# Three edits at three places of an eight-layer transformer kernel: one reciprocal for four heads, the second mixer's decayed scores moved later, and four items between scores and weights in attention

## The chip, the cores and the metric

The kernel is one program on one core of a Trainium2 chip. The metric is the device time of the whole program in microseconds (us), the median over several executions. A core has TensorE (PE, matrix products), VectorE (DVE), ScalarE (ACT), GpSimd (POOL) and SyncE (SP, which here only starts DMAs). Each engine takes its own instructions strictly in order and waits at semaphores for the others.

## The reference

Two stacks run one after the other on 256 tokens of width 1024. The first stack has two layers with 256 context tokens beside the 256 tokens, the second has four layers with 16 meta tokens ahead of them (272 tokens). Everything is float32. The three pieces that matter here, cut to their core:

```python
# first stack, layer 0, differential attention: one square sum over 128 values for each of 4 heads
def diff_post(o, subln_g, lam_init):
    o = rms_norm(o, subln_g, SUBLN_EPS) * (1.0 - lam_init)      # y = x * rsqrt(mean(x^2) + eps) * g

# first stack layer 1 (8 heads x 2 query blocks, 512 keys) and FoX attention (16 heads)
def fox_attend(q, cq, qpos, k, v, ck, kpos):
    s = jnp.einsum('bqhd,bkhd->bhqk', q, k) 
    s = jnp.where(kpos[None, :] <= qpos[:, None], s + (cq[..., :, None] - ck[..., None, :]), -jnp.inf)
    p = jax.nn.softmax(s, axis=-1)
    return jnp.einsum('bhqk,bkhd->bqhd', p, v)

# second stack, layer 1 (GLA): scores with a decay per channel
def gla_chunk(state, inputs):
    b = jnp.cumsum(g, axis=1)
    decay = jnp.exp(jnp.where(causal, b[:, :, None] - b[:, None, :], -jnp.inf))
    A = jnp.einsum('bthd,bshd,btshd->bhts', q, k, decay)
    ...
```

The second stack's layers are FoX, GLA, GDN, FoX, each followed by a gated feed-forward layer.

## The kernel before

The program is a list of stages (classes with one method per engine). Most stages multiply activations by streamed weights: a ring of six 1 MB slots is filled by SP, ACT copies the upper half of each float32 weight (L2034, two halves of 1.0 us), DVE forms the lower half (L2042), and PE does three products for each block (L2069). SP starts a slot's next load when PE has finished with its last content. Between most stages there is a barrier: the next stage's instructions on an engine wait until all three engines are through.

**Head norm.** `HeadNorm` runs after the first layer's attention, on four heads of 128 partitions x 512 tokens. For each head ACT squares (L690), PE sums over the partitions with a 128x128 matrix of ones, so that every partition gets the same row (L708), ACT takes the root (L696), DVE takes the reciprocal of all 128x512 values (L720) and scales the head (L730). Beside it PE and ACT do four slots of the modulation product (`ModSlots`: L409, L418, L436; the DVE ends them with L453 and L459). Then `OutNorm` begins, with ACT's split of the activations (L2129) and of its first weights (L2034, which ACT does ahead of the barrier), and PE's first product (L2069).

**Attention.** `Attention` works through a list of items in steps. An item is a head and a block of queries; it has `maps` (one product q.k, or two for the differential heads). In step i the engines do, each in its own order:

- PE: scores of item i (L803), transposes of the weights of item i-2 (L812), output product of item i-3 (L822);
- DVE: mask and maximum of item i (L857, L860, L869, L877), then reciprocal of the sum and scaling of the weights of item i-1 (L890, L894);
- ACT: exponential of item i (L924), copy of the transposed weights of item i-2 (L934), copy of the output of item i-3 (L940).

PE's scores of item i wait for the exponential of item i-2, since their PSUM banks are shared. Where the next stage is known (`follow`), ACT and DVE also do its splits at fixed steps (L2410, L2405, L2414, and three `upper` of L2034 in steps N-7, N-4 and N-1). There are four such stages: the first layer's (mixed items, with one and two maps), the second layer's (16 equal items of 512 keys), and FoX twice. In the first FoX stage the 48 items repeat in threes (the text calls them M, A and B: 16, 144 and 272 keys, with one, two and three blocks of transposes); in the second one the 32 items alternate A, B.

**GLA.** `GlaProject` multiplies by 12 weight slots, with 28 results (`items` 0 to 27), and hangs other work between them: after result i come `beside_tensor`, `beside_scalar` and `beside_vector` with that i. Results 8 to 19 are the values V, in threes of 16, 128 and 128 tokens, three to a slot. The decayed scores have eight levels, l = -1 to 6. For each level from 0 on DVE forms differences (`diff`, L3087, L3089), ACT exponentials (`decay`, L3013), DVE multiplies q and k by them (`scaled`, L3098), PE multiplies (`pairs`, L2910, L2914, L2917), and DVE keeps what belongs to the level (`kept`, L3110, L3112). The table `SCORES` says after which result a level's `pairs` stands; `diff` and `decay` stand two results ahead of it, `scaled` one ahead, `kept` one behind. `SPLIT_SLOTS` is 3: after the last result of a slot come the splits of the slot three later.

Of the kernel before, what the change touches and what calls it, by code (L numbers as in the profile page):

```python
# [18 lines left out]
ALU = mybir.AluOpType  # L19
# [715 lines left out]

class Attention(Stage):
# [21 lines left out]
    def ahead_scalar(self, act, step):  # L758
# [4 lines left out]
        for k in range(KC):  # L763
            if step == self.done(k) + 5:
# [3 lines left out]
    def ahead_vector(self, dve, step):  # L768
# [4 lines left out]
        for k in range(KC):  # L773
            if step == self.done(k) + 4:
                dve.wait_ge(self.scalar_done, self.act.at("out", self.done(k)))
                self.follow.split_times(dve, k)
            if step == self.done(k) + 6:
                self.follow.split_lo(dve, k)
# [5 lines left out]
    def bank(self, i, m):  # L784
        return (i % 2) * 2 + m
# [4 lines left out]
    def tensor(self, pe):  # L790
        c, N = self.c, len(self.items)
        ident = c.s("ident")
        for step in range(N + 3):
# [12 lines left out]
            if 2 <= step < N + 2:  # L806
                i, it = step - 2, self.items[step - 2]
# [3 lines left out]
                for b, (lo, n) in enumerate(self.blocks(it)):  # L811
                    tr = pe.transpose(c.ps[0:n, 4 + i % 2, b * P:b * P + it["rows"]],  # L812
                                      self.p[0:it["rows"], 2 * (i % 2), lo:lo + n], ident[0:it["rows"], 0:it["rows"]])
                tr.then_inc(self.tensor_done, self.pe.mark("turned", i))
            if step >= 3:
                i, it = step - 3, self.items[step - 3]
# [14 lines left out]
    def vector(self, dve):  # L831
# [5 lines left out]
        for step in range(N + 1):  # L837
            if self.mods and step == self.steps + 2:
                self.mods.finish(dve, self.dve)
            if step < N:  # L840
                i, it = step, self.items[step]
                R, K = it["rows"], it["keys"]
                for m in range(len(it["maps"])):
                    col = self.cols[0:R, self.bank(i, m), :]
                    dve.wait_ge(self.tensor_done, self.pe.at("scores", i, m))
                    if i >= 2:

                        dve.wait_ge(self.scalar_done, self.act.at("exp", i - 2, m if m < len(self.items[i - 2]["maps"]) else 0))
                        dve.wait_ge(self.vector_done, self.dve.at("weights", i - 2))
# [28 lines left out]
            if step >= 1:  # L878
                i, it = step - 1, self.items[step - 1]
# [12 lines left out]
                p0 = self.p[0:R, 2 * (i % 2), 0:K]  # L892
                col = self.cols[0:R, self.bank(i, 0), :]
                ins = dve.tensor_scalar(p0, p0, col[:, 6:7], None, ALU.mult)  # L894
                if M == 2:
                    ins.then_inc(self.vector_done, self.dve.mark("p0", i))
                    p1 = self.p[0:R, 2 * (i % 2) + 1, 0:K]
# [7 lines left out]
        if self.follow:  # L905
            for step in range(N + 1, N + 6):
                self.ahead_vector(dve, step)

    def scalar(self, act):
        c, N = self.c, len(self.items)  # L910
        for step in range(N + 3):
            if step < N:
                i, it = step, self.items[step]
                R, K = it["rows"], it["keys"]
                for m in range(len(it["maps"])):
                    col = self.cols[0:R, self.bank(i, m), :]
                    act.wait_ge(self.vector_done, self.dve.at("neg", i, m))
                    if i >= 2:
                        act.wait_ge(self.tensor_done, self.pe.at("turned", i - 2))
# [4 lines left out]
                    act.activation(self.p[0:R, 2 * (i % 2) + m, 0:K], src, ACT.Exp, bias=col[:, 2:3],  # L924
# [3027 lines left out]
```

## Time and the profile before

| | us |
|---|---|
| median of 3 runs | 3140.18 (3138.24 to 3140.91) |
| the profiled execution | 3141.45 |
| its span in the profile | 3139.6 |
| PE busy | 2833.6 (90%) |
| DVE busy | 2133.0 (68%) |
| ACT busy | 1574.0 (50%) |
| head norm, from its first instruction to PE's first product of the next stage | 22.1 (332.5 to 354.6) |
| second layer's attention | 43.9 (911.9 to 955.8) |
| first FoX attention | 95.8 (1482.2 to 1578.0), PE busy 80.7, DVE 69.3 |
| GLA from result 8 to the state's products | 60.1 (1845.5 to 1905.6), PE busy 48.9 |
| second FoX attention | 75.4 (2840.2 to 2915.6), PE busy 59.3, DVE 53.4 |

The profiled execution took 1.85 us more than its span, which lies around the span, and 1.27 us more than the median. The last five rows are stretches of the span, in us from its start. PE's busy time counts overlapping products, so that 90% is not PE at its peak. The span's forty slices show PE at eight or nine tenths from the seventh slice on, with a few dips; the places of the change lie in slices 5, 12 and 13, 19 to 21, 24 and 25, and 37 and 38.

### The profile page before, as it was taken

How to read it: one execution, taken by the hardware profiler on the slowest of the kernel's cores; microseconds unless marked ns; L12 is line 12 of the kernel's file. 1: busy time of each engine (PE TensorE's matmuls, PEld its weight loads, DVE VectorE, ACT ScalarE, POOL GpSimd, SP SyncE). 2: the span in 40 equal slices, each digit the busy share in tenths (PEclk: the TensorE clock that was granted, in tenths of full speed). 3: DMA queues.
4: the chain of work that ended last, by engine and by line, in shares of the span. 5: the costliest groups of instructions: out<-in, count | busy, mean ns of one | idle time of the engine just before them, and what ended most of it. 6: DMA issues, size and time to landing. Idle time of an engine off the chain costs nothing.

```text
span 3139.6 us, 56486 instructions
## 1 busy us (share of the span) xinstructions
PE 2833.6 (90%) x21486; PEld 2547.6 (81%) x21486; DVE 2133.0 (68%) x3895; ACT 1574.0 (50%) x2757; POOL 94.4 (3%) x92
## 2 busy tenths in 40 slices
PE   6988779997797999789899988999988899998999
PEld 4855559996656999778799978998878799897898
DVE  2167649886475899676767775677746577786676
ACT  3255348775444888654643354434732343455532
POOL 0000001110000011000000000000000000000000
PEclk9999879998798999889999999999989999999999
DMA  8262229999272999933045532454420155441453
GB/s 269 87 201 81 81 100 360 355 353 332 68 228 73 337 355 356 313 95 121 1 135 174 174 95 91 165 174 151 131 81 1 46 169 174 148 130 46 135 187 108
DMA packets 420405, 524.51 MB, mean 167 GB/s; under 512 B 14160, under 2 KB 386912, under 8 KB 419952
## 3 DMA queue, kind: packets, MB, share of 16 engines
q1 hardware_dynamic: 408336, 499.72, 48.1%
q0 software_dynamic: 9216, 12.61, 1.2%
q10 hardware_dynamic: 2656, 9.49, 0.8%
q8 instruction: 132, 2.16, 0.3%
q14 instruction: 65, 0.53, 0.1%
HBM read 521.71 MB, written 21.02 MB: 173 GB/s over the span
## 4 chain that ended last, share of the span: by engine, by line
PE 76%; DVE 10%; ACT 5%; DMA 5%; issue 3%; ACTq 0%; PEldq 0%; SPq 0%; DVEq 0%; PEld 0%; POOLq 0%
PE ps L2069 19%; PE ps L2557 6%; PE ps L2558 6%; PE ps L2559 6%; PE ps L1716 3%; PE ps L1715 3%; PE ps L1714 3%; PE ps L2577 3%; PE ps L2579 3%; PE ps L2578 3%; DMA ring<-in_w_down 2%; PE ps L803 2%; PE ps L822 2%; PE ps L1750 2%; PE ps L1752 2%
## 5 line engine op out<-in xcount | busy, mean ns | idle before, releaser
L1884 DVE TENSOR_TENSOR W_lo<-ring,W_hi 128x1024 fp32r<-128x1024 f32 x384 | 452.5, 1220 | 61.2 <-ACT W_hi L1801 58.4
L2069 PE MATMUL ps<-H_part,W_hi 128*128 128x272 f32 (+2 forms) x1800 | 418.6, 307 | 31.3 <-DVE H_part L1973 12.7
L1801 ACT ACTIVATE W_hi<-ring 128x1024 fp32r<-128x1024 f32 x384 | 385.1, 1053 | 77.8 <-DMA ring<-in_w_up 35.2
L2606 ACT ACTIVATE W_hi<-ring 128x1024 fp32r<-128x1024 f32 x264 | 263.0, 1049 | 293.9 <-PE ps L2579 185.4
L2557 PE MATMUL ps<-room_part,W_hi 128*128 128x272 f32 (+1 forms) x1408 | 404.4, 287 | 5.0 <-DVE room_part L1973 5.0
L2558 PE MATMUL ps<-room_part,W_hi 128*128 128x272 f32 (+1 forms) x1408 | 403.6, 287 | 0.0
L2559 PE MATMUL ps<-room_part,W_lo 128*128 128x272 f32 (+1 forms) x1408 | 402.8, 286 | 0.0
L2069 PEld LDWEIGHTS ps<-H_part,W_hi 128*128 128x128 f32 x1800 | 303.2, 192 | 54.0 <-issue 35.7
L2646 DVE TENSOR_TENSOR W_lo<-ring,W_hi 128x1024 fp32r<-128x1024 f32 x264 | 313.9, 1218 | 10.6 <-ACT W_hi L2606 9.6
L2069 PE MATMUL ps<-H_part,W_lo 128*128 128x272 f32 (+2 forms) x1024 | 305.1, 298 | 0.0
L2042 DVE TENSOR_TENSOR W_lo<-ring,W_hi 128x1024 fp32r<-128x1024 f32 x186 | 219.4, 1220 | 117.3 <-ACT W_hi L2034 116.5
L1714 PE MATMUL ps<-W_hi,A_split_hi 128*128 128x256 f32 x1024 | 293.6, 287 | 2.3 <-DVE A_split_lo L1890 2.3
L1716 PE MATMUL ps<-W_hi,A_split_lo 128*128 128x256 f32 x1024 | 290.5, 284 | 0.0
L1715 PE MATMUL ps<-W_lo,A_split_hi 128*128 128x256 f32 x1024 | 289.9, 283 | 0.0
L2689 DVE TENSOR_TENSOR X<-X,ps 128x272 f32<-128x272 f32 (+1 forms) x352 | 141.0, 428 | 198.5 <-PE ps L2579 196.6
L2557 PEld LDWEIGHTS ps<-room_part,W_hi 128*128 128x128 f32 x1408 | 265.1, 188 | 7.8 <-issue 7.1
L2559 PEld LDWEIGHTS ps<-room_part,W_lo 128*128 128x128 f32 x1408 | 265.1, 188 | 0.0
L2558 PEld LDWEIGHTS ps<-room_part,W_hi 128*128 128x128 f32 x1408 | 265.0, 188 | 0.1
L2034 ACT ACTIVATE W_hi<-ring 128x1024 fp32r<-128x1024 f32 x186 | 185.6, 1049 | 150.5 <-PE ps L2069 121.3
L2577 PE MATMUL ps<-room_part,W_hi 128*128 128x272 f32 (+1 forms) x704 | 205.5, 292 | 21.2 <-DVE W_lo L2646 21.2
L2579 PE MATMUL ps<-room_part,W_lo 128*128 128x272 f32 (+1 forms) x704 | 205.2, 291 | 0.0
L2578 PE MATMUL ps<-room_part,W_hi 128*128 128x272 f32 (+1 forms) x704 | 204.8, 291 | 0.0
(492 smaller groups left out, 6292.4 us busy)
## 6 DMA issues: line engine op xcount, KB each, us to landing
ring<-in_w_down SPq DMA_DIRECT2D x108, 1024.0 KB, 5.0
ring<-in_w_gate_up SPq DMA_DIRECT2D x88, 1024.0 KB, 5.1
ring<-in_w_gate SPq DMA_DIRECT2D x64, 1024.0 KB, 9.8
ring<-in_w_up SPq DMA_DIRECT2D x64, 1024.0 KB, 9.5
ring<-in_w_mod SPq DMA_DIRECT2D x48, 1024.0 KB, 5.8
ring<-in_fox_w_in SPq DMA_DIRECT2D x32, 1024.0 KB, 5.8
ring<-in_gdn_w_in SPq DMA_DIRECT2D x16, 1024.0 KB, 5.7
ring<-in_gla_w_in SPq DMA_DIRECT2D x12, 1024.0 KB, 6.2
```

Source lines behind the costliest of these rows:

```text
L1714: pe.matmul(out, xh, wh[:, k, :], start=(k == 0), stop=False)
L1715: pe.matmul(out, xh, wl[:, k, :], start=False, stop=False)
L1716: mm = pe.matmul(out, xl, wh[:, k, :], start=False, stop=(k == KC - 1))
L1801: act.activation(self.parts(p)[0][:, W], c.ring[:, g % SLOTS, W], ACT.Copy).then_inc(c.hi_done, 1)
L1884: dve.tensor_tensor(lo, c.ring[:, (self.g0 + p) % SLOTS, W], hi.bitcast(F32), ALU.subtract)\
L2069: mm = pe.matmul(self.out(i), a, b, start=(k == 0 and n_part == 0), stop=(k == KC - 1 and n_part == 2))
L2557: pe.matmul(out, wh[:, k, M], hi, start=(k == 0), stop=False)
L2558: pe.matmul(out, wh[:, k, M], lo, start=False, stop=False)
L2559: mm = pe.matmul(out, wl[:, k, M], hi, start=False, stop=(k == KC - 1))
L2577: pe.matmul(out, wh[:, k, M], ah, start=(k == 0), stop=False)
L2579: mm = pe.matmul(out, wl[:, k, M], ah, start=False, stop=(k == 1))
L2646: dve.tensor_tensor(lo, c.ring[:, (self.g0 + p) % SLOTS, C], hi.bitcast(F32), ALU.subtract)\
```

## The change

It does three things.

1. `HeadRoots` takes the place of `HeadNorm` after the first layer's attention. PE sums the squares of the four heads in 32-partition groups with a column of ones, so that one 128x128 tile holds all 4 x 512 sums; one root and one reciprocal of that tile follow; PE spreads the rows again to 128 partitions, four products of 128 columns for each head; DVE scales with the spread values in PSUM.
2. `Attention` gets `depth` and `lag`. Where all items have one map, `depth` is 4 and `lag` is 1: four PSUM banks and four weight buffers, PE's scores of item i wait for the exponential of item i-4, and in step i DVE scales the weights of item i-2 (not i-1), PE transposes those of i-3 (not i-2) and multiplies those of i-4 (not i-3), and ACT copies i-3 and i-4. The splits for the next stage stand one step later, the three `upper` where they were. The first layer's attention has items with two maps and keeps 2 and 0.
3. `GlaProject.SCORES` puts most levels one or two results later, and `diff` and `decay` stand three results ahead of `pairs`, `scaled` two.

```diff
+class HeadRoots(Stage):
+    HEADS, SIDE = 4, 4
...
+    def tensor(self, pe):
+        c = self.c
+        self.mods.tensor(pe, 0, self.HEADS)
+        pe.wait_ge(self.vector_done, self.dve.at("column"))
+        for h in range(self.HEADS):
+            pe.wait_ge(self.scalar_done, self.act.at("square", h))
+            for q in range(self.SIDE):
+                mm = pe.matmul(c.ps[32 * q:32 * q + 32, 0, 0:P], self.column[:, 31 - h:63 - h], self.sq[:, h, q * P:(q + 1) * P],
+                               start=(h == 0), stop=(h == self.HEADS - 1))
+        mm.then_inc(self.tensor_done, self.pe.mark("sums"))
+        self.mods.tensor(pe, 1, self.HEADS)
+        pe.wait_ge(self.vector_done, self.dve.at("root"))
+        for h in range(self.HEADS):
+            for q in range(self.SIDE):
+                one = c.s("ident")[:, 32 * q + h:32 * q + h + 1].to_broadcast([P, P])
+                mm = pe.matmul(c.ps[:, h, q * P:(q + 1) * P], one, self.root, start=True, stop=True)
+            mm.then_inc(self.tensor_done, self.pe.mark("spread", h))
+        self.mods.tensor(pe, 2, self.HEADS)
+        self.mods.tensor(pe, 3, self.HEADS)
+
+    def scalar(self, act):
+        c = self.c
+        for h, x in enumerate(self.heads):
+            act.activation(self.sq[:, h, :], x, ACT.Square).then_inc(self.scalar_done, self.act.mark("square", h))
+        self.mods.scalar(act, 0, self.HEADS)
+        act.wait_ge(self.tensor_done, self.pe.at("sums"))
+        act.activation(self.root, c.ps[:, 0, 0:P], ACT.Sqrt, bias=self.eps, scale=1.0 / (P * self.after ** 2))\
+           .then_inc(self.scalar_done, self.act.mark("root"))
+        for s in range(1, self.HEADS):
+            self.mods.scalar(act, s, self.HEADS)
...
+        dve.reciprocal(self.root, self.root).then_inc(self.vector_done, self.dve.mark("root"))
+        for h, x in enumerate(self.heads):
+            dve.wait_ge(self.tensor_done, self.pe.at("spread", h))
+            dve.scalar_tensor_tensor(x, x, self.gain, c.ps[:, h, :], ALU.mult, ALU.mult)
+        self.mods.finish(dve, self.dve)
...
+        single_maps = all(len(it["maps"]) == 1 for it in items)
+        self.depth, self.lag = (4, 1) if single_maps else (2, 0)
...
     def bank(self, i, m):
-        return (i % 2) * 2 + m
+        return i % 4 if self.depth == 4 else (i % 2) * 2 + m
...
-                if i >= 2:
-                    for m in range(len(self.items[i - 2]["maps"])):
-                        pe.wait_ge(self.scalar_done, self.act.at("exp", i - 2, m))
+                if i >= self.depth:
+                    for m in range(len(self.items[i - self.depth]["maps"])):
+                        pe.wait_ge(self.scalar_done, self.act.at("exp", i - self.depth, m))
...
-    SCORES = {8: -1, 9: 0, 10: 1, 12: 2, 13: 3, 15: 4, 16: 5, 18: 6}
+    SCORES = {9: -1, 11: 0, 12: 1, 14: 2, 15: 3, 16: 4, 17: 5, 19: 6}
...
-        l = self.SCORES.get(i + 2)
+        l = self.SCORES.get(i + 3)
...
-        l = self.SCORES.get(i + 1)
+        l = self.SCORES.get(i + 2)
```

**ACT in the second FoX stage, before.** An exponential (L924), the copy of transposed weights (L934, 256 columns for an item A, 384 for B) and the copy of an output (L940) are a step.

```order
1480 L924 ACTIVATE H,room<-H,room 128x272
1481 L934 ACTIVATE room<-ps 128x384
1482 L940 ACTIVATE room<-ps 64x128
1483 L924 ACTIVATE H,room<-H,room 128x144
1484 L934 ACTIVATE room<-ps 128x256
1485 L940 ACTIVATE room<-ps 64x128
```

And with the change (L987 is the exponential, L998 and L1005 the copies):

```order
1475 L987 ACTIVATE H,room<-H,room 128x144
1476 L998 ACTIVATE room<-ps 128x384
1477 L1005 ACTIVATE room<-ps 64x128
1478 L987 ACTIVATE H,room<-H,room 128x272
1479 L998 ACTIVATE room<-ps 128x256
1480 L1005 ACTIVATE room<-ps 64x128
```

The kinds of instructions stand in the same order as before. What moved is the item behind the exponential: the one of 272 keys is now followed by the copy of an item A, and the one of 144 keys by that of an item B.

**DVE in GLA, before.** It begins with the two instructions that form b (L3075, L3079).

```order
1817 L3075 SCALAR_TENSOR_TENSOR room<-room 128x1088
1818 L3079 SCALAR_TENSOR_TENSOR room<-room 128x1088
1819 L3087 TENSOR_TENSOR room<-room 128x1088 x2
1820 L3098 TENSOR_TENSOR ACC<-room 128x544 x2
1821 L3098 TENSOR_TENSOR ACC<-room 128x272x2 x2
1822 L3110 COPY_PREDICATED room<-ACC,ps 128x256
1823 L3112 COPY_PREDICATED room<-ACC,ps 16x64
1824 L2042 TENSOR_TENSOR W_lo<-ring,W_hi 128x1024 x2
```

And with the change (L3154 `diff`, L3165 `scaled`, L3177 and L3179 `kept`, L2107 the lower half of a weight slot):

```order
1813 L3142 SCALAR_TENSOR_TENSOR room<-room 128x1088
1814 L3146 SCALAR_TENSOR_TENSOR room<-room 128x1088
1815 L3154 TENSOR_TENSOR room<-room 128x1088 x2
1816 L3165 TENSOR_TENSOR ACC<-room 128x544 x2
1817 L2107 TENSOR_TENSOR W_lo<-ring,W_hi 128x1024 x2
1818 L3165 TENSOR_TENSOR ACC<-room 128x272x2 x2
1819 L3177 COPY_PREDICATED room<-ACC,ps 128x256
1820 L3179 COPY_PREDICATED room<-ACC,ps 16x64
```

The differences of levels 0 and 1 and the products of level 0 stand as before, but the weight slot's lower half is now ahead of the products of level 1 and of `kept` of level -1.

**DVE in the head norm with the change** (L786 the reciprocal, L789 the scaling, L453 and L459 the modulation's end); before it were four pairs of L720 and L730, each of 128x512, between L443 and L453.

```order
434 L781 MEMSET ACC 128x63
435 L783 MEMSET ACC 128x1
436 L442 MEMSET ps 128x256 x3
437 L443 TENSOR_REDUCE room<-small 128x2
438 L786 RECIPROCAL ACC<-ACC 128x128
439 L789 SCALAR_TENSOR_TENSOR room<-room,small,ps 128x512 x4
440 L453 TENSOR_TENSOR MOD<-ps,small 128x8 x2
```

One reciprocal of a quarter of the size of one before stands ahead of four scalings, which now read PSUM.

## Rows read from the trace of the kernel before

**Rows 1.** Timeline of the head norm: start us, us, engine, line; idle before in brackets.

```profile
333.79 1.28 ACT L696 ACT_TABLE_LOAD   x1
...
335.81 3.35 DVE L720 RECIPROCAL ACC<-ACC 128x512 f32<-128x512 f32 x1 [2.25 <-ACT ACC L696]
...
339.20 0.75 DVE L730 SCALAR_TENSOR_TENSOR room<-room,small,ACC 128x512 f32<-128x512 f32 x1
...
345.23 2.00 ACT L2034 ACTIVATE W_hi<-ring 128x1024 fp32r<-128x1024 f32 x2 [0.17 <-issue]
...
352.54 4.27 ACT L2129 ACTIVATE H_part<-room 128x512 fp32r<-128x512 f32 x8 [5.31 <-DVEq L3850]
...
354.63 0.77 PE L2069 MATMUL ps<-H_part,W_hi 128*128 128x512 f32 x1 [8.92 <-DVE room_part L2134]
```

**Rows 2.** The reciprocals of line L1085: ns min/median/max, forms.

```profile
L1085 DVE RECIPROCAL stat<-stat x4: 553/753/953, 415.0 to 1343.4; 128x128 f32<-128x128 f32 x2, 128x64 f32<-128x64 f32 x2
```

**Rows 3.** Timeline of PE in the second layer's attention.

```profile
923.45 1.02 PE L803 MATMUL ps<-room 128*128 128x512 f32 x2
...
924.75 1.05 PE L822 MATMUL ps<-room 128*128 128x128 f32 x8
...
925.64 1.02 PE L803 MATMUL ps<-room 128*128 128x512 f32 x2
```

**Rows 4.** Timeline of the second FoX attention, one loop.

```profile
2867.98 0.36 ACT L934 ACTIVATE room<-ps 128x256 f32<-128x256 f32 x1
...
2868.98 0.37 DVE L857 TENSOR_SCALAR H<-ps,room 128x144 f32<-128x144 f32 x1 [0.98 <-PE ps L803]
...
2870.29 0.52 ACT L924 ACTIVATE H<-H,room 128x272 f32<-128x272 f32 x1 [1.49 <-DVE room L877]
...
2870.81 0.47 ACT L934 ACTIVATE room<-ps 128x384 f32<-128x384 f32 x1
...
2871.34 0.94 PE L822 MATMUL ps<-room 128*128 128x128 f32 x6 [0.18 <-ACT room L934]
...
2872.11 0.62 PE L803 MATMUL ps<-ACC,room 128*128 128x272 f32 x2
...
2873.23 0.37 DVE L857 TENSOR_SCALAR H<-ps,room 128x144 f32<-128x144 f32 x1 [0.84 <-PE ps L803]
```

**Rows 5.** Timeline of the first FoX attention.

```profile
1504.40 0.23 DVE L857 TENSOR_SCALAR H<-ps,room 128x16 f32<-128x16 f32 x1
...
1508.66 0.41 PE L803 MATMUL ps<-ACC,room 128*128 128x144 f32 x2
...
1508.86 0.36 DVE L894 TENSOR_SCALAR H<-H,room 128x272 f32<-128x272 f32 x1
...
1509.36 0.23 DVE L857 TENSOR_SCALAR H<-ps,room 128x16 f32<-128x16 f32 x1
...
1510.48 0.23 DVE L894 TENSOR_SCALAR H<-H,room 128x16 f32<-128x16 f32 x1
```

**Rows 6.** Waits of PE over the span: us in total, times, longest.

```profile
PE ps L803 <- ACT H L924: 5.4, 2, 3.2
```

**Rows 7.** Timeline of GLA after result 8.

```profile
1852.19 2.49 DVE L3087 TENSOR_TENSOR room<-room 128x1088 f32<-128x1088 f32 x2
...
1856.25 1.08 PE L2910 MATMUL ps<-ACC 128*32 128x32 f32 x64 [6.73 <-DVE ACC L3098]
...
1863.01 0.41 PE L2069 MATMUL ps<-W_hi,H_part 128*16 128x256 f32 x2
...
1863.74 2.36 DVE L2042 TENSOR_TENSOR W_lo<-ring,W_hi 128x1024 fp32r<-128x1024 f32 x2 [5.56 <-ACT W_hi L2034]
...
1865.83 0.40 PE L2069 MATMUL ps<-W_hi,H_part 128*128 128x256 f32 x2
```

**Rows 8.** Waits of PE in GLA, 1845 to 1910.

```profile
PE ps L2910 <- DVE ACC L3098: 9.4, 3, 6.7
```

**Rows 9.** GLA by stretch: length, busy PE, PEld, DVE, ACT, POOL, granted clock, DMA.

```profile
1857.00:1861.00 4.00, 4.00 (x50) 3.96 (x41) 1.18 (x4) 0.00 (x0) 0.00 (x0) 0.50 0.02 4
```

More of the change, by code:

```diff
@@ L763, in ahead_scalar @@
         for k in range(KC):
-            if step == self.done(k) + 5:
+            if step == self.done(k) + 5 + self.lag:
                 act.wait_ge(self.scalar_done, self.act.at("out", self.done(k)))
@@ L773, in ahead_vector @@
         for k in range(KC):
-            if step == self.done(k) + 4:
+            if step == self.done(k) + 4 + self.lag:
                 dve.wait_ge(self.scalar_done, self.act.at("out", self.done(k)))
                 self.follow.split_times(dve, k)
-            if step == self.done(k) + 6:
+            if step == self.done(k) + 6 + self.lag:
                 self.follow.split_lo(dve, k)
@@ L805, in tensor @@
                     mm.then_inc(self.tensor_done, self.pe.mark("scores", i, m))
-            if 2 <= step < N + 2:
-                i, it = step - 2, self.items[step - 2]
+            i = step - 2 - self.lag
+            if 0 <= i < N:
+                it = self.items[i]
                 pe.wait_ge(self.vector_done, self.dve.at("weights", i))
@@ L812, in tensor @@
                     tr = pe.transpose(c.ps[0:n, 4 + i % 2, b * P:b * P + it["rows"]],
-                                      self.p[0:it["rows"], 2 * (i % 2), lo:lo + n], ident[0:it["rows"], 0:it["rows"]])
+                                      self.p[0:it["rows"], self.bank(i, 0), lo:lo + n], ident[0:it["rows"], 0:it["rows"]])
                 tr.then_inc(self.tensor_done, self.pe.mark("turned", i))
-            if step >= 3:
-                i, it = step - 3, self.items[step - 3]
+            i = step - 3 - self.lag
+            if i >= 0:
+                it = self.items[i]
                 pe.wait_ge(self.scalar_done, self.act.at("turned", i))
@@ L836, in vector @@
             self.mods.begin(dve)
-        for step in range(N + 1):
+        for step in range(N + 1 + self.lag):
             if self.mods and step == self.steps + 2:
@@ L877, in vector @@
                         dve.tensor_scalar(col[:, 2:3], col[:, 0:1], -scale, None, ALU.mult).then_inc(self.vector_done, self.dve.mark("neg", i, m))
-            if step >= 1:
-                i, it = step - 1, self.items[step - 1]
+            i = step - 1 - self.lag
+            if 0 <= i < N:
+                it = self.items[i]
                 R, K, M = it["rows"], it["keys"], len(it["maps"])
@@ L905, in vector @@
         if self.follow:
-            for step in range(N + 1, N + 6):
+            for step in range(N + 1 + self.lag, N + 6 + self.lag):
                 self.ahead_vector(dve, step)
@@ L910, in scalar @@
         c, N = self.c, len(self.items)
-        for step in range(N + 3):
+        for step in range(N + 3 + self.lag):
             if step < N:
@@ L927, in scalar @@
                 self.mods.scalar(act, step - 1, self.steps)
-            if 2 <= step < N + 2:
-                i, it = step - 2, self.items[step - 2]
+            i = step - 2 - self.lag
+            if 0 <= i < N:
+                it = self.items[i]
                 act.wait_ge(self.tensor_done, self.pe.at("turned", i))
@@ L935, in scalar @@
                    .then_inc(self.scalar_done, self.act.mark("turned", i))
-            if step >= 3:
-                i, it = step - 3, self.items[step - 3]
+            i = step - 3 - self.lag
+            if i >= 0:
+                it = self.items[i]
                 act.wait_ge(self.tensor_done, self.pe.at("out", i))
@@ L944, in scalar @@
         if self.follow:
-            for step in range(N + 3, N + 5):
+            for step in range(N + 3 + self.lag, N + 5 + self.lag):
                 self.ahead_scalar(act, step)
@@ L3080, in beside_vector @@
             dve.wait_ge(self.vector_done, self.dve.at("b"))
-        l = self.SCORES.get(i + 2)
+        l = self.SCORES.get(i + 3)
         if l is not None and l >= 0:
```

38 lines of the change are left out of this document (26 added, 12 removed).

## The prediction

> **What bounds the kernel now.** I read the page first: PE is the busiest engine and most of the chain that ended last is on it, so a change pays where PE waits, or where the others make a stage long. Then I asked for the stretches that the change touches (the table's last five rows), and for timeline and waits in each.
>
> In the head norm DVE is the bound: the reciprocal of 128x512 takes 3.35 us, the next scaling 0.75, and a pair starts every 4.05 us ([rows 1]: from 335.81, four pairs). PE's last wait before its first product is 8.92 us and ends with DVE's split.
>
> The second attention is bound by PE: from one item's scores to the next 2.19 us, with no wait [rows 3]. In the second FoX stage nobody is full; there is a loop. Start at the mask of an item B (272 keys), 2868.98: its exponential starts 1.31 us later, then ACT's copy of a B item's weights 0.52 later, PE's output product of that item 0.53 later, the next B item's scores 0.77 later, and DVE's next mask of a B 1.12 after that: 4.25 us for a pair of items [rows 4]. Each link has waited for the one before. The first FoX stage needs 4.96 us for three items (1504.40 to 1509.36, both the first instruction for an item A) [rows 5], and there DVE is almost full. At the start of both stages PE waits for the first exponential, 5.4 us together [rows 6].
>
> In GLA, PE stands 6.73 us before level 0's products, since b and its differences are late: DVE makes two differences from 1852.19 on and only then the products [rows 7]. All three waits of this kind make 9.4 us [rows 8], and behind the first PE goes at the granted clock 0.50 (1.2 of 2.4 GHz) [rows 9].
>
> **The change, part by part.** *Head norm.* Removed: four reciprocals and the tie of each scaling to its own; 4 x 4.05 = 16.2 us of DVE end at about 352.1. Added: four squares in a row on ACT (end about 335.0), 16 small products for the sums. I have no row of that shape here and bound them: 0.9 us if they go like the eight passes of L822 (0.89 [rows 3]), 3.6 if each of 32 passes costs as much as one of those (0.11); I take 1.8, since the output is 32 wide, and they end at 336.9. The root's table load takes 1.28 us and can lie ahead of its wait, as in the head norm now (333.79, before the sums were there) [rows 1]; then the root is done at 337.4, otherwise at 338.7. The reciprocal of 128x128 is the longest of L1085, 0.95 us [rows 2]: 338.4. PE spreads in eight passes per head, 0.89 us each by L822 [rows 3], and DVE's scaling (0.75) keeps up: it ends about 342.9. But now PE has the last two modulation slots *behind* the spreads, about 1.0 us each with 0.6 for the turning products and ACT's copies between, and the stage ends near 346.3 instead of 352.5. ACT's split of the first weights (2.00 us, at 345.23 [rows 1]) was hidden beside the reciprocals; now it ends about 347.3 and the split of the activations starts then, not at 352.54. PE's first product stays 2.1 us behind that. Gain 5.3 us; 3 if the spreads go at the lower clock or the root is late, 8 if the split is hidden and the clock stays up.
>
> *Attention.* It reads like deeper buffering, but I followed the order. In step i PE still does its output product behind the copy that ACT does in step i-1, behind the exponential of i-1, behind DVE's mask of i-1. The lag moves the older items by one, not the steps: no link of the loop goes away. What changes is *which* item is copied and multiplied in a loop, and the start.
>
> Second layer: equal items, so nothing in the middle. PE's third and fourth scores no longer wait at the start: one score (0.86 us, 2.19 less 1.33) and a little at the end. Gain 1.4 (0 to 2.5).
>
> Second FoX stage: behind the exponential of a B now comes the copy of an A (0.36 instead of 0.47 us) and its output product, four passes instead of six (0.45 instead of 0.77; half of 0.89 in [rows 3]). The loop is 4.25 - 0.11 - 0.32 = 3.82 us. DVE needs 3.4 for a pair and PE 3.2, so the loop still decides. Behind the exponential of an A comes the heavier item, but that loop has only 3.4 us. Thirteen pairs between start and end: 13 x 0.43 = 5.6. At the start I followed the first six items: scores of item 5 come 3.1 us earlier; one more step drains at the end, 0.6. ACT's three weight splits keep their steps. Gain 8.1; between 2.5, the start alone, and 10.
>
> First FoX stage: the same shift falls badly. Items come M, A, B. Before, the exponential of a B was followed by copy and product of an M, the lightest; now by those of a B. From the mask of B: 1.31 to the exponential, 0.52, 0.53, then 0.77 for the product [rows 4], then the scores of the next A, whose mask can start 0.70 later (1508.66 to 1509.36 [rows 5]), 3.83 us after the mask of B, where DVE was free at about 3.2. From the mask of A to the weights' scaling 1.12 (1509.36 to 1510.48), the scaling of a B's 0.36 [rows 5]: 5.3 us for three items, and 5.6 in every second three where a split of the next stage (0.43) stands behind it. Against 4.96, about 0.45 x 12 = 5.4 us lost. The start gives back: scores 2 and 3 no longer wait, 4.7 us earlier, of which I keep 3 because PE at 1487 goes at the lower clock before and after; the drain costs 0.8. Sum: 3.2 us slower; 2 faster to 7 slower.
>
> *GLA.* Products of results 10 and 11 move ahead of level 0. A result takes 2.82 us (1863.01 to 1865.83 [rows 7]), so 5.6 of the 6.73 us are filled; the differences start at 1852.19 as before and level 0's multipliers are ready at 1856.2. Then the new order: DVE has slot 7's lower half (2.36 us [rows 7]) ahead of level 1's multipliers. ACT's upper half for it starts near 1856.9, DVE ends it at 1860.3, the multipliers at 1861.7, `kept` of level -1 at 1862.2; PE is ready at 1860.0 and waits 2.3 us, a new wait. Following all steps, the later waits are 0.6, 0.7 and 1.5 us (the last at the state's products, since ACT's copies of the scores now stand behind a weight split). Waits fall from 11.2 (9.4, 1.2 and 0.6) to 6.3, and 2.3 us of lost clock go: 7.2, up to 8.1 by the end times that I get. If the two waits (1.2 and 2.3) drop the clock again, 1 to 2 go back. Gain 7.0; 4 to 8.5.
>
> After the first wait of 6.73 us the clock was granted at half for 4 us [rows 9]. The Trainium skill (TensorE: Matmul & The Clock Gate, "HAM oscillation") says that idle stretches throttle PE again and that it then starts cold, and it holds up shorter, repeated waits as a danger of their own. By this rule the new 2.3 us wait would cost about 2 us of clock; with the row before me I count 1. With the page's reading the sum would be 1 us less.
>
> *The sum:* 5.3 + 1.4 + 8.1 - 3.2 + 7.0 = 18.6 us. From the profiled execution, 3141.45 (span 3139.6 and 1.85 around it), that gives 3122.9; it lies 1.27 above the median, so the median should be 3121.6. The stages behind follow PE and take an earlier start whole: SP's loads are released by PE.
>
> **The rivals.**
> *Deeper buffers help everywhere.* If DVE's wait for exponentials or scores was what held the first FoX stage, it falls to DVE's own work, 4.55 us for three: 12 x 0.4 + 2.2 = 7 us faster instead of 3.2 slower: 3111. For it: scores run less tightly behind exponentials. Against it: in the steady part PE waits for no exponential; the two waits there are stand at the starts [rows 6].
> *Gains lost on the way.* Head norm 3 and GLA 4 as above, second FoX 5 instead of 8: 3140.2 - 3 - 1.4 - 5 + 3.2 - 4 = 3130. For it: the new wait behind slot 7, and modulation slots behind the spreads. Against: both were counted.
> *Nothing moves in the loops.* If the pairing does not matter and only the starts count, FoX gives 2.5 and 2.2: 5.3 + 1.4 + 2.5 + 2.2 + 7 = 18.4: 3122, the same time by another way; only the stages' lengths tell.
> *Slower than before.* One mechanism: each step behind the lag costs, in all 96 steps, since the heavier of two copies always lands in the loop. It decides above (5.3 + 7.0 + the starts' 7) / 96 = 0.20 us per step. In the first FoX stage I expect 0.15; if the same 0.45 per three came in all, it would be 14 us and still not enough; at 0.25 per step 24 us against 19: 3145.
>
> **How the numbers follow.** Forecast 0.70 (the third rival's 0.10 inside it), buffers help everywhere 0.10, gains lost 0.16, slower 0.04 (half of it above 0.2%). Own range of the forecast 3114 to 3129, from adding the parts' bounds halfway. To hold 8 of 10 I take 3112 to 3130. A measurement here tells 0.2%, 6.3 us, from no change: faster is every case but a part of the last two: 0.94, same 0.04, slower 0.02.
>
> **What would show it.** In the profile after: one reciprocal of 0.95 us in the head norm and PE's first product about 348.8 after the span's start. The second FoX stage 67 us instead of 75.4, with 3.8 us from one B's mask to the next; the first about 99 instead of 95.8, with 5.3 or more for three. In GLA a wait of about 1.2 at level 0 and of about 2.3 at level 1, ended by DVE behind L2107. The prediction is wrong if the first FoX stage gets shorter in its middle, if the second does not, or if the waits in GLA come back at later levels.

## The result, and the profile after

The changed kernel takes 3119.62 us (median of 5 runs, 3118.04 to 3125.42) beside 3140.18 before: a ratio of 0.9942, 95% interval 0.9929 to 0.9954, which is 18.2 us less (14.4 to 22.3). The two medians lie 20.6 us apart, within that interval; where the text gives a difference, it is that of the ratio, unless it says otherwise. A median of 3121.6 was forecast. The profiled execution took 3118.04, its span 3116.2.

The total came out, but not all of its terms. I took every instruction that stands in both traces and subtracted its start after from its start before; how much this lead grows over a stage is what the stage gave. The second profile is of the same changed kernel, taken later (`e10` below); in the last column the named experiment has that edit without the other two.

| us gained | forecast | changed | changed, second profile | edit alone |
|---|---|---|---|---|
| first layer's attention, unchanged code, and its end | 0 | 6.0 | 1.5 | |
| head norm up to PE's next product | 5.3 | 6.1 | 6.1 | 6.1 (e1) |
| 10 us behind it | in it | 0.9 | -0.4 | 0.7 |
| second layer's attention | 1.4 | 0.6 | 0.6 | 0.6 (e2); also 0.6 in e1, which has not the edit |
| first FoX stage; 7 us behind it | -3.2 | -1.7; -0.9 | -1.1; -2.2 | +0.2; -0.3 (e2) |
| GLA; the 70 us behind it | 7.0 | 7.3; 1.2 | 8.9; 0.1 | 5.7; 2.7 (e3) |
| second FoX stage; 15 us behind it | 8.1 | 3.9; -2.1 | 4.0; -2.2 | 3.8; -2.1 (e2) |

The stages of the change, with the stretches behind them, make about 15 us and 14 us in the two profiles. The first profile has 6.0 us more, ahead of them, in code that no edit touches. So 3 to 4 of the 18.2 us have no place in the stages of the change; the interval reaches down to 14.4. Below are the windows of the changed kernel that answer to the table of before: length, busy PE, PEld, DVE, ACT, POOL, granted clock, DMA.

```profile
326.40:342.40 16.00, 10.76 (x144) 8.06 (x145) 7.46 (x17) 8.69 (x16) 0.00 (x0) 0.98 0.69 218
897.90:941.30 43.40, 39.19 (x225) 27.48 (x225) 26.73 (x73) 31.42 (x78) 0.00 (x0) 0.96 0.26 83
1467.70:1565.30 97.60, 77.03 (x481) 62.59 (x481) 68.08 (x289) 57.57 (x207) 0.00 (x0) 0.96 0.04 12
1834.10:1887.20 53.10, 48.75 (x790) 44.14 (x789) 40.17 (x52) 30.45 (x51) 0.00 (x0) 0.98 0.30 95
2819.30:2890.70 71.40, 57.90 (x368) 47.40 (x368) 52.93 (x208) 45.62 (x142) 0.00 (x0) 0.98 0.05 16
2890.70:2895.00 4.30, 4.25 (x20) 4.28 (x21) 3.48 (x5) 0.52 (x2) 0.00 (x0) 0.50 0.02 4
```

They were 22.1, 43.9, 95.8, 60.1 and 75.4 us. In the last row PE has just begun the stage behind the second FoX, at half clock (1.2 of 2.4 GHz).

The head norm of the changed kernel, from its timeline (compare [rows 1]):

```profile
328.71 1.06 PE L755 MATMUL ps<-ACC 128*32 128x128 f32 x32
...
329.36 1.28 ACT L774 ACT_TABLE_LOAD   x1
...
330.66 0.37 ACT L774 ACTIVATE ACC<-ps,small 128x128 f32<-128x128 f32 x1
...
331.06 0.95 DVE L786 RECIPROCAL ACC<-ACC 128x128 f32<-128x128 f32 x1 [3.35 <-ACT ACC L774]
332.06 3.84 PE L763 MATMUL ps<-ACC,small 128*128 128x128 f32 x32 [0.90 <-DVE ACC L786]
333.26 3.43 DVE L789 SCALAR_TENSOR_TENSOR room<-room,small,ps 128x512 f32<-128x512 f32 x4 [1.25 <-PE ps L763]
...
339.01 2.00 ACT L2099 ACTIVATE W_hi<-ring 128x1024 fp32r<-128x1024 f32 x2 [0.17 <-issue]
...
342.40 0.76 PE L2134 MATMUL ps<-H_part,W_hi 128*128 128x512 f32 x1 [2.90 <-DVE room_part L2199]
```

One reciprocal of 0.95 us stands where four of 3.35 were. The 32 passes of the sums (two for each of the 16 products) cost 1.06 us together. PE's last wait is 2.90 us instead of 8.92.

The second FoX stage's loop (compare [rows 4]; L919 is DVE's first mask instruction, L987 the exponential, L998 the copy, L884 the output product, L863 the scores):

```profile
2847.48 0.37 DVE L919 TENSOR_SCALAR H<-ps,room 128x144 f32<-128x144 f32 x1 [0.51 <-PE ps L863]
...
2848.80 0.52 ACT L987 ACTIVATE H<-H,room 128x272 f32<-128x272 f32 x1 [1.35 <-DVE room L939]
...
2849.44 0.38 ACT L998 ACTIVATE room<-ps 128x256 f32<-128x256 f32 x1
...
2849.87 0.71 PE L884 MATMUL ps<-room 128*128 128x128 f32 x4
...
2850.42 0.62 PE L863 MATMUL ps<-ACC,room 128*128 128x272 f32 x2
...
2851.54 0.37 DVE L919 TENSOR_SCALAR H<-ps,room 128x144 f32<-128x144 f32 x1 [0.65 <-PE ps L863]
```

The links are the forecast ones, with the lighter item (256 columns, four passes) behind the heavy exponential. Their sum is 4.06 us, not 3.82: exponential to copy 0.64 instead of 0.52, product to scores 0.55 instead of 0.45. Every second time the loop takes 3.93 us. The loop before took 4.25 and 4.39 us in turn; the 4.25 of [rows 4] is one of the two.

PE's waits of the changed kernel in GLA (compare [rows 8]): us in total, times, longest.

```profile
PE ps L2976 <- DVE room L3179: 2.1, 3, 1.7
PE ps L3030 <- ACT room L3108: 1.1, 1, 1.1
PE ps L2976 <- DVE ACC L3165: 1.1, 1, 1.1
```

The waits are 1.1 at level 0, 1.7 at level 1 and 1.1 at the state's products, and 0.4 at later levels; 1.2, 2.3, 1.5 and 1.3 were forecast. The slot that causes the second is seen in the timeline:

```profile
1846.28 2.36 DVE L2107 TENSOR_TENSOR W_lo<-ring,W_hi 128x1024 fp32r<-128x1024 f32 x2 [1.49 <-ACT W_hi L2099]
1848.56 1.35 DVE L3165 TENSOR_TENSOR ACC<-room 128x544 f32<-128x544 f32 x2
...
1850.51 0.72 PE L2976 MATMUL ps<-ACC 128*32 128x32 f32 x62 [1.74 <-DVE room L3179]
```

### The profile page after: what moved, and what is told of

Read it like the earlier page. It is cut to its first block, busy times and chain, and to the rows that moved or that the text cites. A ratio compares the mean times of both kernels' runs of the same rounds, so it can differ in the third digit from the quotient of the medians.

```text
span 3116.2 us, 56580 instructions
## 1 busy us (share of the span) xinstructions
PE 2821.5 (91%) x21542; PEld 2543.4 (82%) x21542; DVE 2122.3 (68%) x3894; ACT 1571.2 (50%) x2754; POOL 93.1 (3%) x92
## 4 chain that ended last, share of the span: by engine, by line
PE 77%; DVE 10%; ACT 5%; DMA 3%; issue 3%; ACTq 0%; PEldq 0%; SPq 0%; DVEq 0%; PEld 0%; POOLq 0%
PE ps L2134 20%; PE ps L2622 6%; PE ps L2623 6%; PE ps L2624 6%; PE ps L1781 3%; PE ps L1780 3%; PE ps L1779 3%; PE ps L2642 3%; PE ps L2644 3%; PE ps L2643 3%; PE ps L884 2%; PE ps L1815 2%; PE ps L1817 2%; PE ps L1816 2%; PE ps L863 2%
## 5 line engine op out<-in xcount | busy, mean ns | idle before, releaser
L2107 DVE TENSOR_TENSOR W_lo<-ring,W_hi 128x1024 fp32r<-128x1024 f32 x186 | 219.6, 1221 | 108.0 <-ACT W_hi L2099 107.6
```

## The experiments

Each kernel is compared by its ratio to the kernel before, run beside it. Where the text says theory A, it means the first of the expectations on record, and B its rival.

**One edit at a time.** The three kernels are the one before with one of the three parts of the diff.

> The kernel before with HeadRoots in the place of HeadNorm and nothing else. In the changed kernel the head norm stage was 6.1 us shorter, and 7.0 us more came from the granted clock in code that the change leaves alone (the first layer's attention and the first products behind the norm). Theory A, the clock there is chance: the stage from its first instruction to the first product of the next stage takes 16 us instead of 22.1, and the median is 6 to 8 us below that of before. Rival B, the clock comes with HeadRoots: the first layer's attention is again about 4.5 us shorter and the median is 13 us lower.

Measured: ratio 0.9971 (0.9961 to 0.9981), 9.1 us less. The head norm stage gave 6.1 us again and the stretch behind it 0.7. The first layer's attention gave nothing and has its half clock as before. Theory A for the stage and the clock; the ratio's 9.1 is 1 us above its 6 to 8. In the profile 3 us or so also came between 400 and 900 us, in code that is the same, so a total of one profile says little here.

> The kernel before with the attention edit alone (depth 4 and lag 1 in the three stages with one map). Theory A, by the stages of the changed kernel: second layer +0.6 us gained, first FoX stage 2.6 lost, second FoX stage 1.7 gained, in all 0.3 us slower (1 faster to 2 slower). Rival B, the sum of the prediction (1.4 - 3.2 + 8.1), with the shorter gain in the changed kernel only a matter of the clock behind the second FoX stage: 6.3 us faster.

Measured: 0.9995 (0.9985 to 1.0005), 1.6 us less with an interval from 4.7 less to 1.6 more. So 6.3 is excluded, the sum that I had forecast for attention; theory A's 0.3 slower lies within the interval.

> The kernel before with the edit to GLA alone. Theory A: the gain is the waits at the first levels and the half clock behind them; 7 to 8.5 us faster, waits for the multipliers fall from 10.6 to about 3 us. Rival B: half of it depends on where the stretch begins, moved by the other edits; 4 us.

Measured: 0.9966 (0.9956 to 0.9975), 10.7 us less (7.9 to 13.8). In its profile GLA gave 5.7 us and the stretch behind it 2.7; the same three waits, 2.1, 1.1 and 1.1 us. Theory A, whose 7 to 8.5 us the interval just reaches; the 4 us of B are excluded. The three ratios multiplied make 0.9932, within the interval of the whole.

**Is the lag what moves the loops, and which way?**

```diff
-        self.depth, self.lag = (4, 1) if single_maps else (2, 0)
+        self.depth, self.lag = (4, 0) if single_maps else (2, 0)
```

> The changed kernel with depth 4 and lag 0 in the three attention stages. Theory A: the lag sets which copy and output product stand in the loop, the banks only fill the start. Then the first FoX stage loses its longer loop (5.37 back to 4.96 us for three items) and keeps the start (4.7 to 6 us): it takes 90 to 92 us instead of 98.4 and the median falls by about 6 us against the changed kernel from there. The second FoX stage goes back to 4.25 us for a pair (from 3.93) and keeps 3 us of start; it has one step less behind the last item: 72 us instead of 71.5 of the changed kernel. In all 5 to 7 us faster than the changed kernel. Rival B, the buffers shape the loop: with four banks and no lag the pair takes 3.93 us and the three items 5.37 as in the changed kernel; no difference to it over 2 us.

Measured: 0.9925 (0.9912 to 0.9939). Time from an item's exponential to that of the item of the same kind behind it, in the steady part of each stage:

| us | first FoX, three items | second FoX, two items | first to last exponential |
|---|---|---|---|
| before | 5.00 and 5.14 | 4.25 and 4.39 | 86.7; 66.6 |
| changed | 5.31 and 5.63 | 3.93 and 4.06 | 85.8; 60.4 |
| four banks, no lag | 5.00 and 5.14 | 4.25 and 4.39 | 82.5; 65.1 |

Banks alone leave the loops as they were and only shorten the start. The first FoX stage gives 4.2 us in place of -2.6 with its stretch behind, the second 1.5. Theory A. By ratio the kernel is 5 us faster than the changed one, with intervals that overlap by 0.001.

```diff
+        self.depth, self.lag = (4, int(len(items) == 32)) if single_maps else (2, 0)
```

> Four banks in all three stages, lag 1 in the second FoX stage alone (32 items), lag 0 in the others. Theory A: lag helps only where two items alternate, so this stage's exponentials go from 65.1 us (first to last, four banks without lag) back to 60.4, one more step drains, and the next stage's first product comes 2.1 us earlier than without lag; the first FoX stage keeps 82.5 us from first to last exponential. Median 0.5 to 2.5 us below that of four banks without lag, depending on whether the 1.6 us of half clock behind the second FoX stage comes. Rival B, the time of the stages also depends on what stands ahead of them (the half clock): the first FoX stage moves by 1 us or more though its code is the same.

Measured: 0.9932 (0.9915 to 0.9948), no better than without lag. The second stage's exponentials did go to 60.4 us and its length fell by 2.5 us more than without lag, but 2.2 us are lost behind it, 0.2 without lag; net 0.5. The first FoX stage gave 2.7 where the same code had given 4.2, with half clock at its end, which e4 had not. So both A (the loop) and B (the clock moves a stage of the same code by 1.5 us) were right.

**Does the neighbour in the loop decide, or the lag as such?** Items of two heads together, no lag:

```diff
+    n = len(items) // 16
+    items = [items[n * (h + j) + t] for h in range(0, 16, 2) for t in range(n) for j in range(2)]
     attention = Attention(c, items, m["p"], m["s"], m["pT"], m["col"])
```

> Four banks, lag 0, and the items of both FoX stages in another order: two heads together, A A B B in the second stage and M M A A B B in the first. Theory A, which copy and output product stand in the loop decides: with A A B B the item two back is of the other kind, so the loop gets the lighter copy behind the heavier exponential without any lag; by the links of the trace (3.93 us for one, 3.45 for the other, in turn) a pair takes 3.7 to 3.9 us where it took 4.32, and from the first to the last exponential 58 to 60 us instead of 65.1. In the first stage three items take 4.7 to 5.0 instead of 5.07. Rival B, lag itself shortens the loop because older items are further back: the order changes nothing, 4.32 and 5.07.

Measured: 0.9908 (0.989 to 0.9925). Four items of the second stage take 7.69 us, 3.84 for two, first to last exponential 59.7; three items of the first stage 4.98. Theory A on every number. The timeline of this kernel shows a heavy exponential (272 keys) with the lighter copy (256 columns) and product (four passes) behind it, without lag:

```profile
2844.15 0.52 ACT L987 ACTIVATE H<-H,room 128x272 f32<-128x272 f32 x1 [1.33 <-DVE room L939]
...
2844.67 0.36 ACT L998 ACTIVATE room<-ps 128x256 f32<-128x256 f32 x1
...
2845.09 0.71 PE L884 MATMUL ps<-room 128*128 128x128 f32 x4
```

**Where the second FoX stage lost its gain.** The lead of the changed kernel over the one before, in us, was 3.0 at item 4's exponential, 4.5 at item 12, 5.8 at item 20, 6.6 at item 26, 6.2 at item 31 (the last), 3.9 at the last copy and at the next stage's first product, and 1.8 some 15 us on. So the loops gave 3.5, the end took back 2.7, and the stretch behind it, at half clock, another 2. All four profiles with the lag and the split in its place (`after`, e2, e5, e10) lose 2.1 to 2.2 us there. e1, e4 and e11, without the lag, lose 0.2 or 0.3, but in e3, whose attention is that of before, and in e6 there is half clock too, and they lose 1.8 and 1.4: the lag is not the only way to it. At the end the timeline of the changed kernel shows a weight split ahead of the copy of item 29:

```profile
2884.30 2.00 ACT L2099 ACTIVATE W_hi<-ring 128x1024 fp32r<-128x1024 f32 x2
...
2886.33 0.49 ACT L998 ACTIVATE room<-ps 128x384 f32<-128x384 f32 x1
...
2886.87 0.94 PE L884 MATMUL ps<-room 128*128 128x128 f32 x6 [1.91 <-ACT room L998]
...
2887.97 2.52 PE L884 MATMUL ps<-room 128*128 128x128 f32 x10
...
2890.75 0.77 PE L2134 MATMUL ps<-room_part,W_hi 128*128 128x256 f32 x2 [0.26 <-issue]
```

```diff
-            if step == N - 7 + 3 * s:
+            if step == (N - 7, N - 4, None)[s]:
                 self.follow.upper(act, s)
...
+        if step == N + 4 + self.lag:
+            self.follow.upper(act, 2)
```

> The changed kernel with its last weight split in attention behind the last copies in place of step N-1. Theory A: in the second FoX stage the exponentials are 6.2 us ahead of the kernel before at the last item and only 3.6 are left at the next stage's first product, because with the lag four items' copies stand behind that split of 2.0 us, and PE stands and falls to the half clock behind it: the stage ends 1.5 to 2.5 us earlier, and the half clock behind it (1.6 us) may go too. Rival B, the loss is the further step of the drain itself: under 0.7 us.

Measured: 0.9913 (0.9897 to 0.9929), 27 us below the kernel before (22 to 32). The second FoX stage gave 5.6 us instead of 3.9, and behind it nothing was lost instead of 2.1. Theory A: the split, not the further step. From the last exponential to the last copy the stage now loses 0.7 us of its lead instead of 2.3, near the 0.6 that I had put down for the further step. The first FoX stage, which has the same edit, came out even in this profile (-2.6 and -3.2 in those of the changed kernel). There was half clock here too, for 3.4 us among the last items (2884.9 to 2888.3), but the first 6 us of the stage behind the second FoX have full clock:

```profile
2889.00:2895.00 6.00, 5.77 (x49) 5.80 (x50) 5.01 (x6) 2.59 (x4) 0.00 (x0) 1.00 0.01 3
```

**Three small moves** on four banks without lag: the split as above, the last two modulation slots ahead of the spreads, and in GLA, for result 10:

```diff
+            if i in self.beside_first:
+                self.beside_vector(dve, i)
             self.move_vector(dve, i)
-            self.beside_vector(dve, i)
+            if i not in self.beside_first:
+                self.beside_vector(dve, i)
```

> Four banks without lag, and three moves in three stages, each read from its own stage. First, in HeadRoots the last two modulation slots stand ahead of the spreads: by the trace PE is idle 0.9 us there and the two slots take 3 us, so the spreads start 2 us later, but nothing of PE stands behind them; the next stage's first product 1.5 to 2 us earlier than in the changed kernel. Second, in GLA the DVE makes the multipliers of level 1 and keeps level -1 ahead of moving result 10 and of slot 7's lower half: the wait of 1.7 us at level 1's products goes, the stretch is 1.5 to 2 us shorter (rival: the delayed lower half of slot 7 makes results wait later, no gain). Third, the last of the three weight splits that ACT does in attention stands behind its last copies, in place of step N-1: PE no longer stands 1 to 2 us between the last items; 1 to 2 us in each FoX stage. In all 4 to 7 us faster than four banks without lag.

Measured: 0.9923 (0.9906 to 0.994); the sum of 4 to 7 did not come. In the head norm 0.6 us more instead of 1.5 to 2: the spreads start 2.6 us later, and the lower half of the first weights (1.23 us), hidden beside ACT before, now stands behind DVE's last scaling. In GLA the wait of 1.7 us is gone:

```profile
PE ps L2984 <- DVE room L3187: 0.6, 2, 0.4
```

and the lead over the kernel without the moves rose by 1.8 us at level 1, but fell by 1.5 at the state's products, because the half clock behind their wait of 1.1 us lasted longer. First the window of this kernel, then that of four banks without lag:

```profile
1873.60:1880.00 6.40, 6.40 (x18) 4.77 (x18) 1.82 (x3) 1.16 (x2) 0.00 (x0) 0.50 0.00 0
```

```profile
1881.10:1884.50 3.40, 3.40 (x12) 2.87 (x11) 1.41 (x3) 0.00 (x0) 0.00 (x0) 0.50 0.00 0
```

The second FoX stage gave 2.7 instead of 1.5, as expected. The first gave 4.2 as without the move: 1.5 us came at its last copies, and half clock among its last items, which e4 had not, took them.

**All moves that helped, and both kernels again.**

> Everything that helped: four banks, lag 0, items by two heads in both FoX stages, the last weight split behind the last copies, the modulation slots ahead of the spreads, level 1's multipliers ahead of slot 7's lower half. Theory A, the stages add up: against the kernel before the head norm 7.0 us, the first FoX stage 3.6 to 4.7, GLA 8.5 to 10, the second FoX stage 5.4 plus 1.2; 25 to 29 us in all in the median, 3112 to 3115 beside a kernel before of 3140. Rival B: the half clock takes the small ones (0.6, 1.2 and 1.5 us) back and the median is that of the items by two heads alone within 1.5 us, 0.991 of the kernel before.

Measured: 3105.28 us, 0.9902 (0.9888 to 0.9917), 31 us below the kernel before run beside it (26 to 35); its median is 14.2 below that of the changed kernel in the next run. The head norm gave 6.8 us, the first FoX stage 6.1, GLA 8.8 and 2.7 behind it, the second FoX stage 8.1 with nothing lost behind: a little more than A's sum. Against 0.9908 for the items by two heads the totals alone don't tell A from B, since the intervals overlap; the stages do, for A.

> The changed kernel unchanged, profiled a second time. Theory A, the half clock in the first layer's attention is chance: its length against the first profile moves by up to 5 us, while every step of the FoX loops (5.30 and 5.63 us for three items, 3.93 and 4.06 for two) and the waits in GLA repeat to 0.05 us. Rival B: the stages all repeat to 0.3 us, and the half clock there belongs to the kernel.

Measured: 3119.52 us, 0.9941 (0.9928 to 0.9955). The first layer's attention up to its last item, 4.4 us shorter than before in the first profile, is as long as before in this one; the loops are 5.31 and 5.63, 3.93 and 4.06. Theory A.

> The kernel before unchanged, profiled a second time. Theory A, the clock there is chance: the first layer's attention may take 4.7 us less than in the first profile, as in five of the eight other kernels, with loops of 4.99 and 5.14 us in the first FoX stage. Rival B: it takes the same 151.5 us within 0.5.

Measured: 3134.92 us in its one run. The first layer's attention took 3.3 us less and its end 1.6 less than in the first profile of the same kernel, the loops were the same to 0.01. Theory A, at 3.3 instead of 4.7. The first row is the first profile of before, the second this one:

```profile
214.00:228.30 14.30, 13.59 (x84) 9.21 (x84) 7.03 (x25) 6.25 (x22) 0.00 (x0) 0.76 0.37 118
```

```profile
214.00:228.00 14.00, 11.98 (x94) 8.13 (x94) 9.54 (x36) 7.98 (x28) 0.00 (x0) 1.00 0.48 158
```

## Why the prediction was right, and where it was not

**The total.** 18.6 us were forecast, 18.2 measured. That they agree so closely is luck. The two profiles give 14 to 15 us for the stages of the change; one term was too large by 6 us, GLA and the head norm gave somewhat more than their terms, and 3 to 4 us of the measured total are not in these stages.

**Head norm, 5.3: right.** From the first square to PE's first product 22.0 us became 15.9. The sums cost 1.06 us, near the lower of the bounds 0.9 and 3.6, of which I had taken 1.8. The reason is not the width of one output: in the trace the passes start in fours, one for each group of 32 rows, 0.007 us apart, and one four follows the other after 0.109 us. The table load was not ahead of its wait but behind the copy of a modulation slot, and still hidden in part; the root was ready 2.3 us behind the last square as forecast (2.4). What bounds the stage now is as forecast: spreads (3.84 for 3.6), then two modulation slots, then ACT's split.

**Second layer, 1.4: the gain was there and was lost at the end.** The stage gave 0.6 us with the edit and also 0.6 in e1 without it, so its length alone shows nothing. Inside the stage the exponentials of the changed kernel are 2.7 us earlier at item 4 and 2.3 at the last item, and at the last copy only 0.6 is left: the split of step N-1 stands ahead of the last copies here too, and PE waits for them. The first row is the changed kernel from 930 to 942 us, the second e8, with the split behind the copies, from 932 to 943:

```profile
PE ps L884 <- ACT room L998: 1.7, 2, 1.3
```

```profile
PE ps L886 <- ACT room L1000: 0.4, 1, 0.4
```

In e8 the lead is 2.3 us at the last exponential and 2.2 at the last copy. Four banks without lag gave 1.2 us in e5 and e6, near the forecast, and nothing in e4, where half clock came 5 us into the stage and took the lead back. PE is the bound in the middle, as forecast.

**First FoX stage, -3.2: right in its loop, and by luck in its sum.** Forecast 5.3 and 5.6 us for three items, measured 5.31 and 5.63. Before they took 5.00 and 5.14 in turn and not 4.96 throughout, so that three items lose 0.40 us and not 0.45. The other terms were off and cancel. Of the start 3 us were kept in the forecast; the lead was 6.2 at item 5 in the first profile and 4.9 in the second. By the last exponential 5.2 and 3.6 of it were gone (5.4 forecast), in the first profile about 1.5 of them at a half clock in the middle that the second does not have:

```profile
1533.10:1536.50 3.40, 3.40 (x15) 3.16 (x14) 1.72 (x7) 1.29 (x7) 0.00 (x0) 0.50 0.00 0
```

Then the end took 2.7 and 2.3 us, where 0.8 was forecast; in e8, with the split moved, it took nothing. The profiles give -2.6 and -3.2 with the stretch behind, two others with the lag (e8, e2) 0 and -0.1. Without its lag the edit would have given 2.7 to 4.2 here (e5, e4).

**Second FoX stage, 8.1: the step that failed.** The mechanism held (e4, e6) and so did the start of 3.1 (measured 3.0). Wrong were, first, the loop, 0.33 for a pair in place of 0.43, and 11 pairs in place of 13, together 3.5 instead of 5.6. Second, and larger, "one more step drains at the end, 0.6" and "ACT's three weight splits keep their steps": with the lag the same step N-1 stands ahead of one more copy, and the split of 2.0 us lies on the path. PE stands 1.9 us and then runs at half clock into the next stage. Measured 2.3 us from the last exponential to the last copy and 2.1 behind; e8 takes the split away and 3.8 us come back. The 1.7 us of these in the stage are the split's; the 2.1 behind it rest on the clock, which e3 and e6 show at half there without the lag. I had followed the loop link by link but not the last four items. The same step of the prediction fails in the other two stages: there the end took 1.7 and 2.3 to 2.7 us.

**GLA, 7.0: right.** It gave 7.3 and 8.9 us. Waits fell from 11.2 to 4.3 us and not to 6.3, the largest difference at level 1 (1.7 for 2.3). Against this the clock fell once more, behind the state's products, in seven of the nine profiles that have this table; in the two others (e8, e10) the stretch gave 8.9 in place of 7.3. I had put the danger at the two first waits. In the changed kernel's profile the clock stayed whole there:

```profile
1840.00:1845.00 5.00, 3.90 (x52) 3.10 (x53) 4.59 (x5) 2.91 (x6) 0.00 (x0) 1.00 0.56 168
1845.00:1850.00 5.00, 3.77 (x96) 3.53 (x88) 3.72 (x5) 2.55 (x4) 0.00 (x0) 1.00 0.14 45
```

but in e3's (and e5's) it was granted at half right behind the wait of level 1, and there GLA gave 5.7 us in place of 7.3:

```profile
1861.00:1864.40 3.40, 3.40 (x17) 3.40 (x18) 3.07 (x6) 2.66 (x5) 0.00 (x0) 0.50 0.02 5
```

The Trainium skill (TensorE: Matmul & The Clock Gate, "A second HAM failure mode: psum-queue depth-cycling", the section behind the one that the prediction names) tells of a kernel in which frequent short idle times let the clock swing; it gives no price for a single wait of 2.3 us. The traces agree in part: behind a wait of 1.7 us the clock fell in two profiles of the seven in which PE waits there, behind the 1.1 us at the state's products in seven of nine, and its price was about 1.6 us each time but one; in e7, where it lasted twice as long, it was 3. I had put 1 to 2 us on it. Part of the price comes back: over the 70 us behind, the profiles with that half clock gain 1.1 to 2.7 us, e8 and e10 0.1, so that GLA and this stretch together give 8.3 to 9.9 us in all but e9 (11.5).

**The rivals.** "Deeper buffers help everywhere" fell with e4 and with the longer loop. "Gains lost on the way" was right for the attention stages, by a mechanism that I had not named. "Nothing moves in the loops" fell: they moved by +0.40 and -0.33 us.

**What stays open:** what decides whether the half clock comes in the first layer's attention. Between 214 and 228 us it came in the first profile of before, in e1, e5 and e10, and not in the other nine, the second one of before among them. That window alone moves an execution by 3.2 us, and the whole stretch up to the head norm moved by 6.0 between two profiles. Open is too why the same wait costs the clock in one profile and not in another, and where the 3 to 4 us of the total lie that the stages do not have.

## What to carry to other kernels

Software pipelining by one more step does not shorten a loop through three engines by itself; it changes which item's work is the neighbour of which, so it helps where heavy and light alternate and harms where the light one was the neighbour already. The order of items does the same without the further step (e6). Work that is hung at a fixed step near the end of a loop has to be checked again whenever the pipeline gets a stage more, with the last items followed one by one: here one split of 2.0 us, left at step N-1, cost 1.5 to 2.9 us in each of three stages.

## What was not expected of the hardware

The granted clock is no constant of the code: stretches with the same instructions had it at 0.76 in one profile and 1.00 in another of the same kernel, and the stage's length went with it by 3 to 5 us. Steps bounded by a loop through several engines repeat to 0.01 us, in stages where PE stands often too. Thirty-two passes of 128 columns into 32 rows took 1.06 us, where 32 passes into 128 rows took 3.84. Each pass is no shorter (0.27 us both); those into 32 rows run four at a time, each into its own 32 of the 128 rows:

```profile
L755 PE MATMUL ps<-ACC x32: 272/273/273, 328.7 to 329.5; 128*32 128x128 f32 x32
L763 PE MATMUL ps<-ACC,small x32: 275/275/376, 332.1 to 335.6; 128*128 128x128 f32 x32
```

The fields are the shortest, median and longest pass in ns, then the starts of the first and the last.
